# Two-block transformer kernel, one core: the boundaries between stages and the linear attention in another order of work

## The chip, the cores and the metric

The kernel runs on one core of one Trainium2 chip. The metric is device microseconds of one execution. The engines have the profile's names: PE is TensorE (matmuls), ACT is ScalarE, DVE is VectorE, POOL is GpSimd, and SP is SyncE, which here issues most of the transfers from HBM.

## What is computed

Two transformer blocks of width 1024 over 512 tokens, batch 1. The first is FFN, gated linear attention beside forgetting attention, FFN; the second is FFN, sparse attention (NSA) beside retention, FFN, with a last norm. Cut to the parts at issue:

```python
def rmsnorm(x, g):
    y = x * lax.rsqrt(jnp.mean(x * x, axis=-1, keepdims=True) + EPS)
    return y * g
def swiglu(h, w_gu, w_dn):
    g, u = jnp.split(h @ w_gu, 2, axis=-1)      # 1024 -> 2 x 2816 -> 1024
    return (jax.nn.silu(g) * u) @ w_dn
# gla_chunked(q, k, v, log_a), of each head and chunk of 64 tokens
    b = jnp.cumsum(gi, axis=2)
    diff = b[:, :, :, None, :] - b[:, :, None, :, :]
    decay = jnp.exp(jnp.where(causal, diff, -jnp.inf))
    A = jnp.einsum('bhtd,bhsd,bhtsd->bhts', qi, ki, decay)
    o = o_inter + jnp.einsum('bhts,bhse->bhte', A, vi)
# token_mixer
    log_a = jax.nn.log_sigmoid(a_low @ w_a2 + b_a) / GLA_TAU
    o_a = rmsnorm(o_a, g_gla) * jax.nn.silu(r_a)
# second_block
    h = h + 0.5 * gt1 * swiglu_2(modulate(rmsnorm_2(h, norm1_w), sh1, sc1), ...)
```

## The kernel before

**Layout and weights.** x is held transposed, 128 partitions x 8 tiles (KT) x 512 tokens; y and xr share its scratch with h_hi and h_lo. The weights come as 420 slabs of 128 x 8 x 128 fp32 (512 KB). A product is made of three passes of fp32r: h_hi by w_hi, h_lo by w_hi, h_hi by w_lo, so 24 matmuls of 512 columns for a slab and a whole output tile. For each slab SP fetches `raw` (`fetch`), ACT rounds it (`high`, L552, writes w_hi), POOL subtracts (`low`, L510, writes w_lo), and PE waits for `lo_done`. All four engines go through the slabs by number, and each waits by a count, so they must agree on the order. There are four buffers in turn (RING), and two spare ones (SPARE) for slabs head+1 and head+2 of each later stage. `freed_by` says which slab must be used up before a buffer is written again.

**Stages.** STAGES = ffn, mix1, ffn, ffn, mix2, ffn. A stage begins with `head` (two slabs k step by k step, as fast as h_hi and h_lo come, for half the tokens, then two more slabs, then the same for the second half), and ends with `out_tiles`: PLAIN[b] = 7 or 6 whole output tiles, three slabs each in an FFN and one in a mix, then the rest in two halves of 256 tokens.

**Boundaries.** Boundary b stands between stage b-1 and stage b. For b = 1, 2, 3 (TWO) the output is first normed (squares in ssacc and sq, summed over partitions on PE by `sum_out`, ACT's square root `std`, DVE's `recip`, PE's `spread` of the result over partitions), added to x (`post`), and the new x is normed again (squares by ACT in y, added up over the eight tiles by POOL's `sum_squares`, L520, one matmul pair for each half in PE's `sum_new`, L1715). Boundaries 4 to 6 have one norm. Then DVE scales x (L1124), ACT makes h_hi (`split_h`, L582), DVE h_lo (L1133). The factors of the modulation (`pre`, DVE L1102 and L1113) are computed at the boundary.

**mix1.** The first slab holds nar: 16 rows for the decay of all heads and 16 for the forget gates. `decay_logits` makes the four heads' logits, ACT copies them with a bias to `lax` (L720) and takes log sigmoid of all four in one piece (L723 to L728, lt). DVE turns them into cumulative sums per chunk (`decay`, L1268 and L1270). A head of the linear attention takes six slabs (gq, gk, two of vt, two of sr, the gate). The decay within a chunk of 128 is factored over seven block sizes (LEVELS): DVE takes differences for each level (`gla_distances`, L1333, L1334), ACT one Exp over all seven (`gla_exponentials`, L783), DVE multiplies by q and k (L1349, L1350), PE makes the scores of one level after the other (L1895), and DVE picks out of each what belongs to the level (L1367, adiag). PE's slabs of the next head stand between those as filler (`interleaved`). The head's output is normed (osq, osum, L1374; PE L1927; ACT L832; DVE L1376) and gated (oa_hi, ACT L837; oa_lo, DVE L1391).

**Order.** Nothing schedules: every engine's program is written out by hand, waits are on semaphores' counts, and each engine works strictly in order. The SP queue carries the slabs in order; in `mix1` and `mix2` ACT issues the constants' transfers.

## Time and profile before

| | us |
|---|---|
| median of 3 runs | 2761.14 (2757.67 to 2764.49) |
| the profiled run's own time | 2758.52 |
| its span | 2756.7 |
| PE busy | 2636.0 (96%) |
| DVE, POOL, ACT busy | 1170.4, 1045.6, 997.9 |
| mean granted clock of PE | 0.976 of full |

The page of the profile gives busy times and shares of the span. Its share for PE says how little is left; where the idle time stands is read from the list of PE's waits, and what the clock was from the table of stretches. A timeline lists one engine's instructions with start and duration; in brackets stands how long the engine had been idle before and what released it.

### The profile page before, as it was taken

To read this page: it belongs to the slowest core of one execution; us is meant where nothing else is said; L and a number is where in the kernel's file an instruction comes from. 1 tells how busy PE (TensorE), PEld (TensorE's weight loads), DVE (VectorE), ACT (ScalarE), POOL (GpSimd) and SP (SyncE) were. 2 spreads that over 40 slices of the span, in tenths; PEclk is the share of its full clock that TensorE was granted. 3 is DMA by queue.
4 is the path that set the end of the run, shared out by engine and by line. 5 is a ranking of instruction groups with operands and counts; after the bars stand their busy time and mean duration, and the time that the engine had idled before them with its cause. 6 is when DMAs were issued, how large, how long until landed. Compare 5 with 4: busy or idle time off the path is not lost.

```text
span 2756.7 us, 36017 instructions
## 1 busy us (share of the span) xinstructions
PE 2636.0 (96%) x12868; PEld 2135.4 (77%) x12868; DVE 1170.4 (42%) x2091; ACT 997.9 (36%) x1577; POOL 1045.6 (38%) x460
## 2 busy tenths in 40 slices
PE   6999997999999999999998999999999999999998
PEld 4788886777777688888888888888666667888887
DVE  6645225665444225644315553122444456522212
ACT  4222335343454444333324322222454335322221
POOL 0444452233333245444444544452121224344443
PEclk9999997999999899999999999998999999999999
DMA  6655331112222234355532554332111222232332
GB/s 262 213 187 197 126 107 42 54 62 78 84 84 84 79 97 138 115 193 196 175 106 87 191 195 137 100 121 77 44 43 61 83 71 92 77 98 92 99 106 93
DMA packets 78569, 313.31 MB, mean 114 GB/s; under 512 B 9072, under 2 KB 11888, under 8 KB 69008
## 3 DMA queue, kind: packets, MB, share of 16 engines
q1 hardware_dynamic: 64368, 234.91, 25.8%
q10 hardware_dynamic: 14112, 77.17, 7.9%
q8 instruction: 61, 1.00, 0.2%
q14 instruction: 28, 0.23, 0.0%
HBM read 309.91 MB, written 2.13 MB: 113 GB/s over the span
## 4 chain that ended last, share of the span: by engine, by line
PE 79%; DVE 11%; issue 6%; ACT 3%; DMA 1%; POOL 1%; ACTq 0%; DVEq 0%; SPq 0%; POOLq 0%
PE bank L1689 22%; PE bank L1691 22%; PE bank L1690 22%; PE bank L1728 2%; PE bank L1730 1%; PE bank L1729 1%; DVE h_lo L1133 1%; PE pair L1961 1%; PE bank L1971 1%; PE bank L2116 1%; PE bank L1979 1%; DVE adiag L1367 1%; DVE lev L1349 1%; ACT h_hi L582 1%; PE bank L2100 1%
## 5 line engine op out<-in xcount | busy, mean ns | idle before, releaser
L510 POOL TENSOR_TENSOR w_lo<-raw,w_hi 128x1024 fp32r<-128x1024 f32 x414 | 1014.6, 2453 | 1649.6 <-ACT w_hi L552 1589.5
L1689 PE MATMUL bank<-h_hi,w_hi 128*128 128x512 f32 x2064 | 834.9, 405 | 25.1 <-DVE lev L1350 11.5
L552 ACT ACTIVATE w_hi<-raw 128x1024 fp32r<-128x1024 f32 x420 | 444.4, 1059 | 1140.1 <-PE bank L1691 1105.6
L1691 PE MATMUL bank<-h_hi,w_lo 128*128 128x512 f32 x2064 | 807.4, 391 | 0.0
L1690 PE MATMUL bank<-h_lo,w_hi 128*128 128x512 f32 x2064 | 806.3, 391 | 0.0
L1689 PEld LDWEIGHTS bank<-h_hi,w_hi 128*128 128x128 f32 x2064 | 390.3, 189 | 120.0 <-issue 16.5
L1691 PEld LDWEIGHTS bank<-h_hi,w_lo 128*128 128x128 f32 x2064 | 388.9, 188 | 83.1
L1690 PEld LDWEIGHTS bank<-h_lo,w_hi 128*128 128x128 f32 x2064 | 390.0, 189 | 77.6 <-issue 4.1
L1689 PE MATMUL bank<-act_hi,w_hi 128*128 128x512 f32 x616 | 239.6, 389 | 0.0
L1690 PE MATMUL bank<-act_lo,w_hi 128*128 128x512 f32 x616 | 239.6, 389 | 0.0
L1691 PE MATMUL bank<-act_hi,w_lo 128*128 128x512 f32 x616 | 239.6, 389 | 0.0
L1235 DVE TENSOR_TENSOR prod<-bank,rstd 128x512 f32<-128x512 f32 x87 | 60.1, 691 | 412.9 <-PE bank L1691 407.9
L1239 DVE TENSOR_TENSOR act_lo<-prod,act_hi 128x512 f32 (+1 forms) x88 | 178.7, 2031 | 84.8 <-ACT act_hi L677 84.8
L1087 DVE SCALAR_TENSOR_TENSOR adaw<-adaw,silu_c 128x1024 f32<-128x1024 f32 x128 | 178.1, 1426 | 3.9 <-DMA adaw<-ada_dram 3.9
L1182 DVE TENSOR_TENSOR ssacc<-ssacc,sq 128x512 f32<-128x512 f32 x34 | 84.8, 2493 | 206.6 <-ACT sq L599 206.5
L1728 PE MATMUL bank<-h_hi,w_hi 128*128 128x256 f32 (+1 forms) x360 | 116.5, 324 | 28.7 <-DVE h_lo L1645 15.2
L1689 PEld LDWEIGHTS bank<-act_hi,w_hi 128*128 128x128 f32 x616 | 115.6, 188 | 24.2
L1691 PEld LDWEIGHTS bank<-act_hi,w_lo 128*128 128x128 f32 x616 | 115.6, 188 | 24.0
L1690 PEld LDWEIGHTS bank<-act_lo,w_hi 128*128 128x128 f32 x616 | 115.6, 188 | 23.7
L1729 PE MATMUL bank<-h_lo,w_hi 128*128 128x256 f32 (+1 forms) x360 | 111.5, 310 | 0.0
L1730 PE MATMUL bank<-h_hi,w_lo 128*128 128x256 f32 (+1 forms) x360 | 111.2, 309 | 0.0
L1728 PEld LDWEIGHTS bank<-h_hi,w_hi 128*128 128x128 f32 x360 | 73.7, 205 | 41.8 <-DVE h_lo L1133 19.3
(387 smaller groups left out, 3085.7 us busy)
## 6 DMA issues: line engine op xcount, KB each, us to landing
raw<-slabs_dram SPq DMA_DIRECT2D x420, 512.0 KB, 3.5
adaw<-ada_dram ACTq DMA_DIRECT2D x62, 1024.0 KB, 6.9
ada<-ada_dram SPq DMA_DIRECT2D x8, 1024.0 KB, 20.3
x<-xt_dram SPq DMA_DIRECT2D x4, 512.0 KB, 7.8
adaw<-ada_dram SPq DMA_DIRECT2D x2, 1024.0 KB, 24.4
fneg<-fneg_scratch ACTq DMA_DIRECT2D x4, 512.0 KB, 3.5
sq<-fneg_scratch ACTq DMA_DIRECT2D x4, 512.0 KB, 3.4
w<-w_dram ACTq DMA_DIRECT2D x1, 2048.0 KB, 8.6
```

What stands on the lines that cost most here:

```text
L510: nc.gpsimd.tensor_tensor(wl[s][:], raw[s][:], wh[s][:], ALU.subtract).then_inc(lo_done, 1)
L552: nc.scalar.activation(wh[s][:], raw[s][:], ACT.Copy).then_inc(hi_done, 1)
L1087: V.scalar_tensor_tensor(rows, rows, 1.0, silu_c[:, b], ALU.mult, ALU.mult, accum_out=mod[:].rearrange("p b j -> p (b j)")[:, ds(at, 1)])\
L1182: V.tensor_tensor(ssacc[:], ssacc[:], sq[:, t % 2], ALU.add).then_inc(ssadd, 1)
L1235: V.tensor_tensor(prod[:], (acc[(m + 1) % 2] if n else bank(m + 1))[:], sg[:], ALU.mult)\
L1239: V.tensor_tensor(act_l[:, ds(j, 1)].rearrange("p a t -> p (a t)"), prod[:], act_h[:, ds(j, 1)].rearrange("p a t -> p (a t)"), ALU.subtrac ...
L1689: MM(out, wh[s][:, k], a, start=first and j == 0, stop=False)
L1690: MM(out, wh[s][:, k], b, start=False, stop=False)
L1691: ins = MM(out, wl[s][:, k], a, start=False, stop=end and j == len(tiles) - 1)
L1728: MM(out, wh[s][:, k], a, start=start, stop=False)
L1729: MM(out, wh[s][:, k], b, start=False, stop=False)
L1730: return MM(out, wl[s][:, k], a, start=False, stop=stop)
```

## The change

A. `EARLY` and `order()`: slabs head+1 and head+2 of each later stage are fetched, rounded and subtracted before the last six slabs of the stage ahead, where that is an FFN, and before its last two, where it is a mix. Their places in the count move with them.

B. POOL adds the new squares of tiles 0 to 4 (four adds instead of seven, each half), and PE sums the rest: eight matmuls of one column instead of two.

C. At boundaries 1 to 3 PE's sum for the second half of the out norm, and its spread, move from ahead of the head into its k loop. ACT's squares, splits and square roots are put in another order to fit, DVE's `pre` goes to the start of `out_tiles`. At the other boundaries `split_h` goes ahead of the slab rounding and the sums come some groups later.

D. Start of mix1: gq comes right after nar; head 0's log sigmoid is done alone and first, the other three heads' later, its scans between the picks; the constants of both mixes are issued by SP between two slabs.

E. The seven levels have a count each: seven Exps of 512 elements instead of one of 3584, DVE and PE wait for each level. In a head, DVE computes osum before the next head's distances, and ACT the next head's Exps after the square root instead of before it.

F. In mix2 DVE waits for the constants after ks_lo instead of before.

```diff
+EARLY = {c: 2 if kind.startswith("mix") else 6 for (_, c, _, _), (kind, _, _, _) in zip(plan(STAGES)[0][1:], plan(STAGES)[0])}
+def order(c, n=0):
...
+    for head, early in EARLY.items():
+        if head - early <= c <= head:
+            return c + SPARE
+        if head < c <= head + SPARE:
+            return c - 1 - early
+    return c
...
             def sum_squares(b, half):
-                hc, done = halves(half), 14 * (b - 1) + 7 * half
-                for n in range(KT):
+                hc, done = halves(half), 8 * (b - 1) + 4 * half
+                for n in range(KT - 3):
...
                 if TWO[b]:
-                    now = 5 if per > 1 else 4
+                    now = KT if per > 1 else 5
                     new_squares(b, 0, range(now))
-                    out_halves(b, c, m, 1)
...
+                    std(ev + 1, 4)
+                    if per > 1:
+                        out_halves(b, c, m, 1)
+                    split_h(b, 0, range(0, 3))
+                    std(ev + 2, 2)
+                    split_h(b, 0, range(3, 5))
                     high(c + 3)
-                    split_h(b, 0)
+                    split_h(b, 0, range(5, KT))
                     new_squares(b, 1)
...
             def sum_new(b, half):
...
+                for n in src:
+                    pe.wait_ge(sx_done, 8 + 16 * (b - 1) + 8 * half + n + 1)
...
                 if TWO[b]:
-                    sum_out(b, 1)
-                    spread(ev + 1, 2, ST)
                     sum_new(b, 0)
-                    spread(ev + 2, 4, SC1)
+                    spread(ev + 1, 4, SC1)
...
+                        if half == 0 and TWO[p] and k == 1:
+                            sum_out(p, 1)
+                        if half == 0 and TWO[p] and k == 5:
+                            spread(ev + 2, 2, ST)
...
+            def gla_exponentials(i, levels=range(len(LEVELS))):
+                for l in levels:
+                    act.wait_ge(g_lev_diff, len(LEVELS) * i + l + 1)
+                    nc.scalar.activation(lev[:, l], lev[:, l], ACT.Exp).then_inc(g_lev_exp, 1)
...
                 if ahead:
+                    gla_exponentials(i + 1, range(0, 4))
                     gla_key(c + 6, m + 6, i + 1)
+                    gla_exponentials(i + 1, range(4, len(LEVELS)))
...
-                if ahead:
-                    gla_distances(i + 1)
                 dve.wait_ge(g_osq, 2 * i + 2)
                 if i:
                     dve.wait_ge(g_osum, i)
                 V.tensor_tensor(osum[:], osq[:, 0], osq[:, 1], ALU.add).then_inc(g_osum, 1)
+                if ahead:
+                    gla_distances(i + 1)
...
             def mix2(c, m, _):
-                dve.wait_ge(m2_in, 96)
                 dve.wait_ge(n_kh, 1)
                 V.tensor_tensor(ksl[:], bank(m + 2)[:], ksh[:], ALU.subtract).then_inc(acc_free[m % 2], 1)
+                dve.wait_ge(m2_in, 96)
```

How the order moves at three places (numbers behind tile names are buffers). ACT at the boundary from the first FFN to mix1, before: the last output tile's second half (the second L620), the eight squares of the new x (y<-x, L630), the three square roots (L574), and the head's rounding.

```order
L620 ACTIVATE sq<-bank 128x256 [waits half_done,ssadd]
L623 ACTIVATE y<-bank,small 128x256
L574 ACTIVATE small<-bank,small 128x2 [waits s_sum]
L630 ACTIVATE y<-x 128x256 [waits x_done] x5
L620 ACTIVATE sq<-bank 128x256 [waits slab_done]
L623 ACTIVATE y<-bank,small 128x256
L630 ACTIVATE y<-x 128x256 [waits x_done] x2
L574 ACTIVATE small<-bank,small 128x2 [waits s_sum]
L630 ACTIVATE y<-x 128x256 [waits x_done]
L574 ACTIVATE small<-pair,small 128x2 [waits s_sum]
L552 ACTIVATE w_hi_59<-raw_57 128x1024 [waits raw_in1]
```

The same place after:

```order
L661 ACTIVATE y<-x 128x256 [waits x_done] x8
L602 ACTIVATE small<-bank,small 128x2 [waits s_sum]
L651 ACTIVATE sq<-bank 128x256 [waits slab_done]
L654 ACTIVATE y<-bank,small 128x256
L610 ACTIVATE h_hi<-pair,mod 128x256 [waits u_done]
L610 ACTIVATE h_hi<-bank,mod 128x256 [waits u_done]
L610 ACTIVATE h_hi<-pair,mod 128x256 [waits u_done]
L602 ACTIVATE small<-bank,small 128x2 [waits s_sum]
L610 ACTIVATE h_hi<-bank,mod 128x256 [waits u_done]
L610 ACTIVATE h_hi<-pair,mod 128x256 [waits u_done]
L580 ACTIVATE w_hi_59<-raw_57 128x1024 [waits raw_in1]
```

All squares of the new x and their square root now stand ahead of the out tile's second half; that half's square root and the rounding stand within the split. PE at the same boundary, before: the sum of the out norm's second half (L1706), its spread (L1723), the sum of the new squares (L1715), its spread, the head's first matmul.

```order
L1706 MATMUL bank<-ones,ssacc 128x1 [waits sqh_done,ssadd]
L1706 MATMUL bank<-ones,sq 128x1
L1706 MATMUL bank<-ones,ssacc 128x1
L1706 MATMUL bank<-ones,sq 128x1
L1723 MATMUL bank<-ident,small 128x128 [waits rcol_done]
L1723 MATMUL bank<-ident,small 128x128
L1715 MATMUL pair<-ones,y 128x1 [waits sx_added]
L1715 MATMUL pair<-ones,y 128x1
L1723 MATMUL pair<-ident,small 128x128 [waits rcol_done]
L1723 MATMUL pair<-ident,small 128x128
L1728 MATMUL bank<-h_hi,w_hi_56 128x256 [waits lo_done,h_done]
```

After:

```order
L1765 MATMUL bank<-ones,y 128x1 [waits sx_done,sx_added]
L1765 MATMUL bank<-ones,y 128x1
L1765 MATMUL bank<-ones,y 128x1 [waits sx_done]
L1765 MATMUL bank<-ones,y 128x1
L1765 MATMUL bank<-ones,y 128x1 [waits sx_done]
L1765 MATMUL bank<-ones,y 128x1
L1765 MATMUL bank<-ones,y 128x1 [waits sx_done]
L1765 MATMUL bank<-ones,y 128x1
L1773 MATMUL pair<-ident,small 128x128 [waits rcol_done]
L1773 MATMUL pair<-ident,small 128x128
L1778 MATMUL bank<-h_hi,w_hi_56 128x256 [waits lo_done,h_done]
```

Eight one-column matmuls over four tiles of squares stand where two over the added-up tile stood, and the out norm's sum and spread are gone from here; they now follow the second and the sixth k step of the head. ACT at the start of mix1, before: from the logits of all heads to the levels' Exp.

```order
L723 ACTIVATE lt_104<-lax 128x2048 [waits la_x]
L724 ACTIVATE lt_104<-lt_104 128x2048 [waits act_chain]
L725 ACTIVATE nar<-nar 16x512 [waits act_chain]
L726 ACT_TABLE_LOAD
L726 ACTIVATE lt_104<-lt_104 128x512 [waits act_chain]
L727 ACTIVATE lt_104<-lt_104 128x1536
L728 ACTIVATE nar<-nar 16x512
L699 ACTIVATE gq<-bank 128x512 [waits slab_done]
L552 ACTIVATE w_hi_59<-raw_57 128x1024 [waits raw_in1,slab_done]
L699 ACTIVATE vt<-bank 128x512
L783 ACT_TABLE_LOAD
L783 ACTIVATE lev<-lev 128x3584 [waits g_lev_diff]
```

After, two pieces of the same place:

```order
L740 ACTIVATE nar<-bank 48x512 [waits slab_done]
L734 ACTIVATE gq<-bank 128x512 [waits slab_done]
...
L748 ACTIVATE lax<-pair,cols 128x512 [waits la_ready]
L752 ACTIVATE lt_104<-lax 128x512 [waits la_x]
L753 ACTIVATE lt_104<-lt_104 128x512 [waits act_chain]
L754 ACT_TABLE_LOAD
L754 ACTIVATE lt_104<-lt_104 128x512 [waits act_chain]
...
L823 ACTIVATE lev<-lev 128x512 [waits g_lev_diff] x7
L828 ACTIVATE eq<-cs 128x512
L830 ACTIVATE ek<-cs 128x128 x4
L769 ACT_TABLE_LOAD
L769 ACTIVATE lt_104<-lt_104 128x1536
```

gq and head 0's log sigmoid moved to the front, the levels' Exp comes in seven, and the log of the other heads stands behind it, with a table load of its own.

## Rows read from the trace of the kernel before

**Rows 1.** The page: busy time of each engine, and SP's fetches (KB each, us to landing).

```profile
PE 2636.0 (96%) x12868; PEld 2135.4 (77%) x12868; DVE 1170.4 (42%) x2091; ACT 997.9 (36%) x1577; POOL 1045.6 (38%) x460
...
raw<-slabs_dram SPq DMA_DIRECT2D x420, 512.0 KB, 3.5
```

**Rows 2.** PE's waits: what it waited for, us in total, times, longest us.

```profile
PE bank L1689 <- DVE lev L1350: 11.5, 2, 10.3
PE bank L1728 <- DVE h_lo L1133: 11.1, 9, 1.6
...
PE pair L1927 <- DVE osum L1374: 5.3, 4, 1.9
PE bank L1689 <- ACT gq L699: 5.2, 1, 5.2
...
PE bank L1689 <- DVE ks_lo L1441: 2.8, 1, 2.8
```

**Rows 3.** Stretches: us, busy PE, PEld, DVE, ACT, POOL (instructions), clock, DMA share, GB/s.

```profile
402.70:429.30 26.60, 19.49 (x126) 18.35 (x125) 14.11 (x39) 12.21 (x29) 9.66 (x11) 0.81 0.08 28
429.30:497.20 67.90, 52.06 (x265) 43.33 (x266) 37.31 (x74) 34.12 (x43) 13.76 (x6) 0.82 0.16 50
...
2366.80:2389.50 22.70, 18.58 (x132) 18.61 (x133) 10.83 (x22) 6.12 (x14) 4.58 (x2) 0.85 0.16 47
```

**Rows 4.** Timeline of PE at boundary 1: start, us, instruction [idle before <-releaser].

```profile
406.39 0.60 PE L1715 MATMUL pair<-ones,y 128*128 128x1 f32 x4 [0.82 <-POOL y L520]
...
410.17 0.58 PE L1728 MATMUL bank<-h_hi,w_hi 128*128 128x256 f32 x1 [1.61 <-DVE h_lo L1133]
```

**Rows 5.** Timeline of POOL at boundary 1.

```profile
403.88 2.45 POOL L520 TENSOR_TENSOR y<-y 128x256 f32<-128x256 f32 x3 [1.80 <-ACT y L630]
```

**Rows 6.** Timeline of ACT at the start of mix1.

```profile
440.79 1.26 ACT L720 ACTIVATE lax<-pair,cols 128x512 f32<-128x512 f32 x2
...
450.51 1.91 ACT L723 ACTIVATE lt<-lax 128x2048 f32<-128x2048 f32 x1
...
455.05 1.28 ACT L726 ACT_TABLE_LOAD   x1
...
459.02 0.60 ACT L699 ACTIVATE gq<-bank 128x512 f32<-128x512 f32 x1
...
466.53 3.20 ACT L783 ACTIVATE lev<-lev 128x3584 f32<-128x3584 f32 x1 [4.04 <-DVE lev L1334]
```

**Rows 7.** Timeline of DVE at the start of mix1.

```profile
457.81 1.23 DVE L1270 TENSOR_TENSOR_SCAN lac<-segm,lt 128x512 f32<-128x512 f32 x1
...
460.88 2.59 DVE L1333 TENSOR_TENSOR lev<-cs 128x256 f32<-128x256 f32 x1
463.40 0.41 DVE L1334 TENSOR_TENSOR lev<-cs 128x256 f32<-128x256 f32 x1
463.73 0.41 DVE L1333 TENSOR_TENSOR lev<-cs 128x256 f32<-128x256 f32 x1
```

**Rows 8.** Timeline of PE at the start of mix1.

```profile
459.67 0.79 PE L1689 MATMUL bank<-h_hi,w_hi 128*128 128x512 f32 x1 [5.19 <-ACT gq L699]
...
485.00 1.05 PE L1895 MATMUL pair<-lev 128*128 128x128 f32 x8
```

**Rows 9.** Timelines of PE and ACT in head 1's second part (osum, oa_hi).

```profile
563.60 1.13 PE L1927 MATMUL pair<-osum,ones 128*128 128x512 f32 x2 [1.11 <-DVE osum L1374]
...
571.84 1.24 ACT L837 ACTIVATE oa_hi<-og 128x512 fp32r<-128x512 f32 x2 [3.46 <-DVE og L1386]
```

**Rows 10.** Timelines of POOL, DVE and PE at boundary 5.

```profile
2361.51 7.52 POOL L510 TENSOR_TENSOR w_lo<-raw,w_hi 128x1024 fp32r<-128x1024 f32 x3 [3.04 <-ACT w_hi L552]
...
2364.39 2.37 DVE L1102 TENSOR_TENSOR mod<-mod,cols 128x16 f32<-128x16 f32 x1
...
2370.92 0.56 PE L1706 MATMUL bank<-ones,ssacc 128*128 128x1 f32 x2 [4.12 <-ACT sq L620]
```

**Rows 11.** Timeline of ACT at boundary 4.

```profile
1856.60 1.06 ACT L552 ACTIVATE w_hi<-raw 128x1024 fp32r<-128x1024 f32 x1 [5.85 <-DMA raw<-slabs_dram]
```

200 lines of the change are left out of this document (112 added, 88 removed).

## The prediction

> **What bounds the kernel now.** I read first the page's line of busy times [rows 1]: PE (TensorE) is busy 2636.0 of 2756.7 us, 96%. So a change can win at most the 121 us in which PE stands still, plus what PE loses where the granted clock is below full. The second view is PE's waits [rows 2]: they are small and stand where a stage begins. Two belong to the start of the linear attention (11.5 for the levels, 5.2 for the query), one to the boundaries between stages (h_lo, 11.1), one to the linear attention's heads (osum, 5.3), one to the start of mix2 (2.8). The third view is the busy time by stretches [rows 3]: the first boundary and the start of mix1 run at a granted clock of 0.81 and 0.82, the boundary before the last FFN at 0.85, so behind an idle PE come matmuls at the lower of its two levels, 1.2 GHz instead of 2.4. A stall there costs its own length and some more. Everything the diff edits lies in such places; elsewhere PE is fed and stays fed.
>
> **Boundaries 1 to 3 (two norms; parts B and C of the change).** Before, PE's last output tile is followed by seven POOL adds for the new squares; the last three take 2.45 us [rows 5], PE waits 0.82 for them before its sum at 406.39, then comes the spread, and the head's first matmul starts at 410.17 after 1.61 more of waiting on h_lo [rows 4]. After, the first half's squares are complete before the last output tile ends: POOL adds four and not seven, and PE goes straight to its sum. The POOL adds (2.45), the sum of the out norm and the second spread leave that path: 2.4 to 3.2 us. What comes in their place: PE's sum is 8 matmuls where there were 2 (the four records of the row at 406.39 took 0.60, so 16 records about 1.9: +1.3); the spread of the out norm now sits in the head's k loop, and ACT's square root for it stands ahead of split tile 3, so ACT waits until PE has done the first two k steps (six matmuls of 256 columns each; +1.6 at full clock, +3.6 at the lower); a reciprocal (+0.15), and the slab rounding of 1.06 [rows 11], now in the middle of the split (tiles 3 and 4 ahead of it). Second half: three POOL adds less (2.6 by the same row), 1.3 of matmuls more. A boundary gives between -1.0 and +1.3. The clock, low there before, decides which. I take 0 for the three together, with -4 to +4 as the bounds.
>
> **Early slabs (part A).** The roundings of slabs head+1 and head+2 (1.06 on ACT [rows 11], 7.52 for three or 2.5 on POOL [rows 10]) move from the end of the out tiles to before the last six slabs (FFN) or two (mix). They lie there beside PE-bound slabs: ACT is busy 36%, POOL 38% [rows 1]. The cost is zero as long as SP's two fetches have landed, for ACT works in order and its next rounding queues behind. If that cover is gone it costs what the transfer is late. SP's queue: the two spare fetches wait for nothing now, and go ahead of the last ones. Gain: boundary 5, below; at boundary 4 ACT waited 5.85 for a raw slab and the split stood behind it [rows 11]. Split now goes first, and of that about 1.6 us was on PE's path: **-1.6**. (End of the kernel: the same freed order, -0.5, bounds -1 and 0.)
>
> **Start of mix1 (parts D and E), the largest term.** ACT before: the squashing of all four heads' gate logits in one piece of 2048 elements, 1.91 for Abs and as much for Exp, then a table load of 1.28, and only then the log of head 0, gq at 459.02, while PE waits 5.19 for gq [rows 6, 8]. DVE's scan of head 0 starts at 457.81 [rows 7]; its 14 level differences follow at 0.34 us a piece (463.40 to 463.73), one of them held to 2.59; ACT's one Exp over seven levels starts at 466.53 and takes 3.20 [rows 6]. DVE meanwhile does the other heads' logs and scans, then the 14 products, and PE gets the levels after 10.3 of waiting, the longest of that group [rows 2]; its third score (the row of eight records) is at 485.00 [rows 8].
> After, step by step from the same durations, a piece of 512 elements on ACT being 0.6 as gq's was [rows 6]: gq directly after nar, so PE doesn't wait for it (5.19 gone). The first logits stand at 440.79 [rows 6]; logit, Abs, Exp, load and Ln of head 0 alone are 0.6 x 4 + 1.28, with gq ahead done at 444.8. DVE: log 0.7, scan 1.23, a copy, so the first pair of differences at 447.9 and, 14 by 0.34, the last at 452. ACT: three more logits, then the first value tile when PE has it, about 450.7 (it stood just ahead of the row at 450.51). Abs and Exp of the other three heads by three quarters of 1.91 each, a load, three pieces for the forget gate: 457.1. Rounding and second value tile: 458.7. Seven Exps of 512 elements, 0.57 each (3.20 in one before, +0.8), until 462.7, each released to DVE as it is done; eq and the four pieces of ek until 464.5; DVE's work from there to the first pick (qp, kp, the chunk tiles, two vtok copies, a pick) about 4.5. The third score comes at about 469.1 and not 485.0: -15.9. Against this: the other heads' logs and scans (three scans of 1.23 and a log of 1536 elements, some 5.4 of DVE) are now between the picks, of which about 1 stays on the path, and one POOL roundings' collision with DVE more, +1. Sum **-14**, with -11 and -18 as ends. From the other side: the two stalls are 15.5, some 3 us of lower clock go with them, and I expect PE to stand about 4 at the first pick.
> The table loads are where a page speaks against this change. Here a load took 1.28 us [rows 6], and the new order makes one more of them (Ln, Exp, Ln); the first is hidden, by the sum above, since PE's slabs bound ACT until 450.7. The Trainium skill, page "ScalarE: Activation LUTs", section "Table sets: the hidden batching unit", puts a switch at about 2.7 us and wants work batched by set; by that figure two loads ahead of the levels would lose up to 2.8 more and the term be -11, an estimate from the page. The trace's 1.28 disagrees, and the measurement decides.
>
> **Heads 1 to 3 (part E).** osum goes ahead of the next head's distances on DVE: PE waited for it four times, 5.3 us in all [rows 2], 1.11 in the second head [rows 9]; three of these go, -3.3. Head 1 gets its scan earlier, -2.0. Against it: the next head's Exps now stand between the square root and oa_hi on ACT, in which ACT before only waited 3.46 for og [rows 9]; DVE's lo part waits on oa_hi, and its products wait for nothing that it doesn't do itself. Levels 0 to 3, gk, 4 to 6, eq, ek are about 6.7 us in a gap of 3.5 plus 2: the first pick comes about 1.0 later in each of heads 2 and 3, and 1.0 in the last: +3. PE then waits about 3 us at a pick; if its clock falls behind that, 2 to 3 us more in each head, which I put at +4 in all. Sum **+2**, ends -2 and +9.
>
> **Start of mix2 (parts D and F).** DVE waited for the constants' transfer before ks_lo, and PE 2.8 for that [rows 2]. Now the wait stands behind ks_lo, and the transfers are issued by SP between its fetches of slabs first+5 and first+6. In SP's queue they stand behind a fetch whose buffer is free once the last out tile is done, long before ks_lo, and the two fetches behind them come six small issues later, with five slabs of PE's time still ahead of them: **-2.8**, ends -2.8 and 0. The same holds for mix1's two (lmask, segm), which ACT issued before. What is queued behind the moved wait is the compression's cab, needed much later.
>
> **Boundary 5.** DVE's small adds of the modulation, one of 16 columns for 2.37 us [rows 10] and one of 8 behind it, ran beside three roundings of POOL back to back (7.52 [rows 10]); they held back the new x, its squares, and PE's sum, for which PE waited 4.12 [rows 10]. Now pre() stands at the start of the out tiles and the spare roundings are done early. PE's sum moves from its second to its sixth group and no longer waits: -4.1, and of the lower clock in this stretch (22.7 us at 0.85 [rows 3]) about 2.1: **-6.2**, ends -4 and -7.
>
> **Sum.** 0 - 1.6 - 0.5 - 14 + 2 - 2.8 - 6.2 = -23.1. The profiled run took 2758.52 (span 2756.7), so 2735.4 by its own measure; the three runs' median is 2761.14, 2.6 above it, which gives **2738**.
>
> **Rivals.**
> A, more than forecast: the boundaries' -1.0 each holds, the lower clock there goes too (a stretch of 26.6 us at 0.81 at boundary 1 [rows 3]; 1 us each of it), and mix1 gives -18: boundaries three times -2, so -6; mix1 -4; heads at -2 instead of +2, -4; 14 less, 2724, and with the kernel's end at -1, 2723. For it: a stall that goes takes low clock with it. Against: the new sums keep a gap of some 4 us at each boundary.
> B, the heads take it back: pick chain +1 to +2 a head and three low-clock stretches (+9), mix1 only -11: 10 more than forecast, 2748. For it: ACT's added 6.7 us stand on the way to oa_hi, and PE's waits there were short before.
> C, slower: DVE and POOL exclude each other. A difference of 256 columns took 2.59 where its neighbours take 0.34 [rows 7], an add of 16 columns 2.37 [rows 10]: each time a rounding ran on POOL. In the new order DVE has its level work strewn through the whole head, six roundings fall into a head, and each could land on the path: four more collisions in each of 4 heads at 2.3 are +36.8, so 2738 + 36.8 = 2775. It decides from 14 collisions more than now (2761 + 8.3 - 2738 = 31 us, over 2.3). Against: DVE's work is the same number of instructions, and only those ahead of a pick count; before, about two of six collide.
> The Trainium skill, page "SBUF — State Buffer", section "Who interferes with whom", says that VectorE and GpSimd share a port pair as an exclusive lock, held for the whole instruction by whoever began. The trace's 2.59 agrees.
> D, the early roundings starve a mix tail: ACT would wait in order for spare slabs; a fetch takes 3.5 us in the median (the row of raw), and PE 2636.0/420 = 6.3 us a slab [rows 1], so three in a row could be late; 5 us at each of the five boundaries would give 2763, no change. Against: six slabs of lead in the FFN tails; only the two mix tails are tight.
>
> **How the numbers follow.** Forecast 0.57, A 0.17, B 0.18, C 0.03, D 0.05. The range takes A and B in: 2723 to 2753 (B with boundaries at +4), and leaves out about 0.2. About 0.3%, 8.3 us, is what a measurement can tell from no change; the forecast, A and B (2748 is -0.5%) are all faster, less a tail of B: faster 0.91, within it 0.06 (D and that tail), slower 0.03 (C).
>
> **What would show it.** In the profile after: PE's wait on gq gone, and that on the levels 4 us or less instead of 11.5; the third score some 14 us earlier against the stage's start than now; ks_lo's wait gone; no wait on the squares at boundary 5 and its granted clock near 1; at boundaries 1 to 3 the stretch from that sum to the head's first matmul much as before (3.8), no wait for POOL ahead of it, but a wait for h_lo at the third or fourth tile; in heads 1 to 3 no wait on osum, one on adiag of about 3 us instead. It is wrong if DVE has many more level instructions of over 2 us than now (C), or ACT idles on raw slabs in a mix tail (D).

## The result, and the profile after

| | before | changed |
|---|---|---|
| median, us | 2764.49 (5 runs, 2757.67 to 2769.85) | 2737.11 (5 runs, 2734.56 to 2739.73) |
| ratio | | 0.991 (0.9893 to 0.9927) |
| the profiled run's own time | 2758.52 | 2737.11 |
| span | 2756.7 | 2735.3 |
| PE busy | 2636.0 (96%) | 2642.1 (97%) |

Forecast were 2738 and a gain of 23.1 us in the profiled run; it was 21.4. The page of the changed kernel, its line of busy times (before: [rows 1]):

```profile
PE 2642.1 (97%) x12940; PEld 2145.9 (78%) x12940; DVE 1156.3 (42%) x2091; ACT 1001.9 (37%) x1604; POOL 1037.2 (38%) x442
```

PE's waits in the changed kernel (waited for: us in total, times, longest; before: [rows 2]):

```profile
PE pair L1948 <- DVE adiag L1413: 15.9, 4, 5.8
PE bank L1778 <- DVE h_lo L1693: 14.0, 7, 7.3
PE bank L1778 <- DVE h_lo L1172: 12.0, 11, 1.6
...
PE pair L1980 <- DVE osum L1420: 1.9, 1, 1.9
```

The waits on the levels (11.5), on gq (5.2) and on ks_lo (2.8) are gone, that on osum fell from four times to one. A new one heads the list: 15.9 us for DVE's picks; before, the picks made PE wait three times for some 4 us in all.

Where the time went can be read more sharply than from the medians. Both kernels run the same 10728 slab matmuls in the same order, so a stretch can be cut from the start of one matmul to the start of another, the same two in both traces. The stretches of the kernel before (window: us, busy PE, PEld, DVE, ACT, POOL with instructions, granted clock, DMA share, GB/s): boundary 1 from the last out tile's second half to the matmul behind the decay logits; from there to the slab matmul behind head 0's cross terms, with four groups of scores still to come; the rest of head 0 and heads 1 to 3; the FFN behind boundary 2 with boundary 3; the start of mix2; the end of mix2 with boundary 5.

```profile
395.65:443.65 48.00, 40.51 (x264) 35.48 (x262) 24.77 (x67) 23.00 (x49) 18.95 (x18) 0.88 0.19 61
443.65:488.60 44.95, 29.50 (x134) 25.39 (x133) 27.98 (x52) 21.68 (x24) 7.42 (x3) 0.75 0.11 35
488.60:643.12 154.52, 144.55 (x765) 120.54 (x763) 108.79 (x190) 64.96 (x85) 51.78 (x18) 1.00 0.19 62
1125.65:1500.66 375.01, 368.81 (x1774) 311.50 (x1774) 158.69 (x206) 118.76 (x165) 177.53 (x82) 0.99 0.46 157
1862.23:1890.89 28.66, 24.86 (x189) 22.27 (x189) 10.05 (x25) 11.50 (x21) 5.42 (x3) 1.00 0.36 126
2042.76:2383.74 340.98, 326.78 (x1576) 239.12 (x1575) 172.48 (x329) 141.41 (x247) 107.54 (x44) 0.97 0.24 78
```

The same six in the changed kernel:

```profile
398.75:444.19 45.44, 41.31 (x286) 37.39 (x284) 24.85 (x67) 22.19 (x49) 12.91 (x11) 0.92 0.19 64
444.19:474.08 29.89, 25.52 (x133) 22.42 (x133) 24.75 (x48) 24.64 (x34) 7.47 (x4) 0.89 0.16 53
474.08:633.05 158.97, 147.39 (x765) 124.74 (x763) 111.24 (x195) 66.44 (x103) 54.46 (x18) 0.97 0.18 60
1115.30:1489.84 374.54, 370.75 (x1797) 313.33 (x1798) 158.54 (x206) 118.64 (x165) 172.56 (x76) 1.00 0.45 157
1849.34:1874.69 25.35, 24.46 (x190) 22.13 (x188) 8.65 (x21) 11.19 (x20) 7.82 (x4) 1.00 0.35 128
2028.22:2362.14 333.92, 323.86 (x1576) 236.29 (x1575) 166.00 (x325) 139.72 (x244) 105.74 (x43) 0.98 0.24 79
```

| place | forecast, us | measured, us |
|---|---|---|
| boundaries 1, 2, 3 | 0 (-4 to +4) | -2.6, +0.3, -0.5 (the last with the FFN ahead of it): -2.8 |
| start of mix1, to the slab matmul behind head 0's cross terms | -14 (-18 to -11) | -15.1 |
| rest of head 0, heads 1 to 3 | +2 (-2 to +9) | +4.4 |
| boundary 4 | -1.6 | -2.1 |
| start of mix2 | -2.8 | -3.3 |
| boundary 5 | -6.2 (-7 to -4) | -7.1 |
| end | -0.5 | -0.3 |
| where nothing was moved | 0 | +3.1 ahead of boundary 1, -0.6 in mix1's second part, +1.7 in mix2's middle, +0.5 behind the last slab |

The cut between boundary 4 and mix2 lies inside the head: 0.5 of the 3.3 us is still boundary 4's, and 2.8 is the wait for ks_lo.

The last row is what one execution differs from another by: a lower clock that came at a place or didn't. The stretch ahead of boundary 1 took 369.6 to 372.4 us in the profiles of the kernel before and two kernels near it, and 370.1 to 373.7 in those of the changed kernel and ten near it. Without this row the edits gave -26.3, against -23.1 forecast and -27.4 between the medians. What the boundaries' row owes to the same spread is told in the part on why the prediction was right.

### The profile page after: what moved, and what is told of

Read it like the earlier page. It is cut to its first block, busy times and chain, and to the rows that moved or that the text cites. A ratio compares the mean times of both kernels' runs of the same rounds, so it can differ in the third digit from the quotient of the medians.

```text
span 2735.3 us, 36041 instructions
## 1 busy us (share of the span) xinstructions
PE 2642.1 (97%) x12940; PEld 2145.9 (78%) x12940; DVE 1156.3 (42%) x2091; ACT 1001.9 (37%) x1604; POOL 1037.2 (38%) x442
## 4 chain that ended last, share of the span: by engine, by line
PE 85%; DVE 7%; issue 5%; ACT 3%; POOL 0%; DMA 0%; DVEq 0%; ACTq 0%; POOLq 0%
PE bank L1737 23%; PE bank L1739 23%; PE bank L1738 22%; PE bank L1778 2%; PE bank L1779 2%; PE bank L1780 2%; PE pair L1948 1%; PE pair L2014 1%; PE bank L2024 1%; PE bank L2032 1%; PE bank L2169 1%; DVE h_lo L1172 1%; DVE lev L1397 1%; DVE lev L1396 1%; PE bank L2153 1%
## 5 line engine op out<-in xcount | busy, mean ns | idle before, releaser
L1275 DVE TENSOR_TENSOR prod<-bank,rstd 128x512 f32<-128x512 f32 x87 | 60.1, 691 | 417.4 <-PE bank L1739 411.7
```

The lines of the kernel that those rows point to most:

```text
L1275: V.tensor_tensor(prod[:], (acc[(m + 1) % 2] if n else bank(m + 1))[:], sg[:], ALU.mult)\
```

## The experiments

Twelve kernels, on the same measure: by place, against the kernel before or the changed one. For the start of mix1 I read the distance from the first decay logit to the last score of head 0 (the matmul of gq and gk): 439.20 to 494.25 in the kernel before, so 55.0, and in the changed kernel 39.2 by these rows of PE's timeline:

```profile
440.56 1.98 PE L1886 MATMUL pair<-nar,wa 16*128 16x512 f32 x4
...
461.12 1.07 PE L1948 MATMUL pair<-lev 128*128 128x128 f32 x8
462.73 1.06 PE L1948 MATMUL pair<-lev 128*128 128x128 f32 x8
468.85 2.04 PE L1948 MATMUL pair<-lev 128*128 128x128 f32 x8 [4.37 <-DVE adiag L1413]
...
479.73 1.05 PE L1948 MATMUL pair<-gq,gk 128*128 128x128 f32 x8
```

**One Exp for seven levels.** Rival theories: the levels in turn carry the gain, or the early start of head 0's chain does.

```diff
                 for l in levels:
-                    act.wait_ge(g_lev_diff, len(LEVELS) * i + l + 1)
-                    nc.scalar.activation(lev[:, l], lev[:, l], ACT.Exp).then_inc(g_lev_exp, 1)
+                    if l == 0:
+                        act.wait_ge(g_lev_diff, len(LEVELS) * (i + 1))
+                        nc.scalar.activation(lev[:], lev[:], ACT.Exp).then_inc(g_lev_exp, len(LEVELS))
```

> The changed kernel with one edit undone: ACT takes the seven levels in one Exp of 3584 elements again, after all differences, in every head. I read the stretch from the decay logits' first matmul to the last score of head 0 (the one of gq and gk): 55.0 us in the kernel before, 39.2 in the changed one. Theory (the time of mix1's start came from starting head 0's chain earlier, and the levels in turn are worth little, because DVE's differences are done at 455.6 and ACT is free for the Exps only at 458.3, so all a single Exp loses is the overlap of DVE's products with it): the products begin about 2.5 us later, the last score 1 to 2 us later, 40 to 41. Rival (the levels in turn are what carries the gain): 45 or more. In heads 1 to 3 both expect little, up to 1 us a head, for the levels' Exps there are hidden beside the normalisation. Whole run +1 to +3 us by the theory, +8 or more by the rival.

Measured: 440.86 to 484.69, 43.8 us, so 4.7 more, between what the two said; 2739.9 us in one run. The Exp starts at 458.58 and takes 3.19, as I had it; the third score is only 3.5 later against the logits (31.8 instead of 28.3). The remaining 1.2 lie behind a wait of 6.51 us: two groups of scores at the lower clock (2.05 and 1.91 us, where 1.05 is the normal; in the changed kernel, behind 4.37 us, it is 2.04 and 1.15):

```profile
472.66 2.05 PE L1949 MATMUL pair<-lev 128*128 128x128 f32 x8 [6.51 <-DVE adiag L1414]
475.79 1.91 PE L1949 MATMUL pair<-lev 128*128 128x128 f32 x8
479.93 1.05 PE L1949 MATMUL pair<-lev 128*128 128x128 f32 x8
```

**The four heads' log sigmoids together.**

```diff
-                logits(0)
-                act.wait_ge(la_x, 1)
...
-                for h in range(1, HG):
+                for h in range(HG):
                     logits(h)
...
-                chain.link(nc.scalar.activation(lt4[:, 1:HG], lax[:, 1:HG], ACT.Abs))
-                chain.link(nc.scalar.activation(lt4[:, 1:HG], lt4[:, 1:HG], ACT.Exp, scale=-1.0))
+                chain.link(nc.scalar.activation(lt4[:], lax[:], ACT.Abs))
+                chain.link(nc.scalar.activation(lt4[:], lt4[:], ACT.Exp, scale=-1.0))
...
+                nc.scalar.activation(lt4[:, 0], lt4[:, 0], ACT.Ln, bias=1.0).then_inc(la_l, 1)
```

> The changed kernel with one edit undone: the log sigmoids of the four heads are taken together again, after the first value tile; gq stays early and the levels stay in turn. Theory (head 0's log alone is the largest piece): its log is ready at about 457 instead of 446, the first difference at 459.5, and from there the pipelined levels need some 13 us to the first pick, so the last score of head 0 comes 4 to 6 us later: 43 to 45 us from the logits instead of 39.2. Rival (the gain is all in not waiting for gq): within 1 us of 39.2. Rival with the levels in turn as the carrier: also within 2 us.

Measured: 438.98 to 489.68, 50.7 us: 11.5 more, twice what I expected; 2745.42 us. Against the logits DVE's first log is 12.3 us later (17.9 instead of 5.6 behind them). In the changed kernel DVE waits 2.8 us for the first Exp, and that is all the slack there is: 9.5 come through, and the lower clock behind PE's waits (7.79 for the levels, 3.74 at the third score) goes with the rest. I had assumed 5 to 7 us of slack.

**gq late.**

```diff
-                gla_query(c + 1, m + 1, 0, ahead=False)
...
                 c, m = c + 1, m + 1
+                gla_query(c, m, 0, ahead=False)
                 gla_value(c, m, 0, 1)
```

> The changed kernel with one edit undone: ACT takes gq out of its bank only after the first value tile and the other heads' Exp, as before, so PE cannot begin the second value slab until then. Theory: PE waits 3 to 5 us for the bank at the second value slab, whose tile then comes as much later; ACT's level Exps stand behind that tile, so the whole chain moves by it: last score 42 to 44 us from the logits instead of 39.2. Rival (that wait was in the shadow of the levels' chain and giving it up costs nothing, since PE waits for the first pick anyway): 39 to 40.

Measured: 442.35 to 482.79, 40.4 us: 1.3 more; 2740.8 us, with 1.8 of the difference standing already ahead of the logits, most of it in boundary 1's head at a clock of 0.76. PE waits 3.19 for the bank, just as expected, and then doesn't wait at the first pick at all (4.37 in the changed kernel). That is close to the rival's 39 to 40 and not the theory's 42 to 44: with the other edits in place that wait stood in the shadow of DVE's chain. In the prediction I had credited it with 5.2 us in my check of the sum.

**The other heads' scans ahead of head 0's products.**

```diff
+                nc.scalar.activation(lt4[:, 1:HG], lt4[:, 1:HG], ACT.Ln, bias=1.0).then_inc(la_l, 1)
+                nc.scalar.activation(nar[32:48, :], nar[32:48, :], ACT.Ln, bias=1.0).then_inc(la_l, 1)
                 c, m = c + 1, m + 1
                 gla_value(c, m, 0, 1)
                 gla_exponentials(0)
...
-                gla_head(c, m, 0, True, others())
+                for _ in others():
+                    pass
+                gla_head(c, m, 0, True)
```

> The changed kernel with one edit undone: the other heads' logs are taken on ACT ahead of the second value tile, and DVE makes their logs and scans ahead of head 0's products, as before, instead of between the picks. Theory (5.4 us of DVE and some 4.5 of ACT with a table load go back onto the chain; part of it runs side by side): last score 45 to 46 us from the logits instead of 39.2. Rival (it was hidden where it stood): within 1.5 us of 39.2. If the four undone edits together give back clearly more than 15.9 us, they overlap and no single one can be credited with the gain.

Measured: 439.73 to 488.83, 49.1 us: 9.9 more; 2750.14 us. More than expected again, and again with waits of 5.68 and 3.68 and the lower clock behind them. Taken singly the four edits give back 4.7 + 11.5 + 1.3 + 9.9 = 27.4 us where all together won 15.9. So none of them owns the gain: they shorten one chain (logits, log, scan, differences, Exp, products, cross terms, first pick), and each of them missing puts back what it saves of that chain, less the slack in it. Where PE's wait grows, matmuls at the lower clock follow (1.2 us with one Exp, some 2 with the logs together). No run has any of the four alone in the kernel before.

**Boundary 5, DVE's additions alone**, in the kernel before:

```diff
             def out_tiles(b, c, m, per, pieces=()):
+                if b < LAST:
+                    pre(b)
...
             def boundary(b, c, m, per):
                 ev = EVENTS[b]
-                if b < LAST:
-                    pre(b)
```

> The kernel before with one part of the change alone: DVE's additions for the modulation move from the boundary to the start of the out tiles; nothing else. Theory (at the boundary before the last FFN these two small additions, 2.4 and 2.3 us beside POOL's roundings, held back the new x and with it PE's sum): PE's wait of 4.1 us there shrinks to at most 1.5, and the same matmuls behind it come 3 to 6 us earlier against the kernel before, with the lower clock in that stretch gone. Rival (POOL's three roundings in a row, which stay where they are in this kernel, hold back DVE's next additions instead): 0 to 2 us, PE still waits 2.5 or more. Elsewhere no change.

Measured: PE's wait there went from 4.12 to 1.16, and the matmuls behind it came 4.4 us earlier (2.9 late ahead of it, 1.5 early once the half is done, by the same matmuls in both traces). Elsewhere differences came and went with the clock, the largest 3.2 us in the middle of mix2 (0.90 against 0.92). One run gave 2758.17, beside 2759.14. The new x starts at once after PE has ended its half, though POOL's three roundings stand there as before:

```profile
2364.40 7.52 POOL L510 TENSOR_TENSOR w_lo<-raw,w_hi 128x1024 fp32r<-128x1024 f32 x3 [3.04 <-ACT w_hi L552]
...
2369.02 0.88 DVE L1195 SCALAR_TENSOR_TENSOR x<-bank,small,x 128x256 f32<-128x256 f32 x2 [1.66 <-PE bank L1730]
...
2370.85 0.35 PE L1706 MATMUL bank<-ones,ssacc 128*128 128x1 f32 x2 [1.16 <-ACT sq L620]
```

**Boundary 5, the sum's place alone**, in the kernel before:

```diff
-                                if half and done == 2:
+                                if half and done == (2 if TWO[b] else 6):
                                     sum_out(b, 0)
-                                if half and done == 5:
+                                if half and done == (5 if TWO[b] else 9):
                                     spread(ev, 0, SC1)
```

> The kernel before with another part alone: at the boundaries with one norm PE's sum of the first half's squares stands behind its sixth group of matmuls instead of its second, the spread behind the ninth instead of the fifth. Theory: four groups of three matmuls of 256 columns are 1.4 us of work that PE does instead of waiting, so its wait at the boundary before the last FFN goes from 4.1 to 2.5 to 3, and 1.5 to 2.5 us are won there. Rival (the place of the sum is what mattered there, and the clock stays up once the wait is short): 4 us or more. At the boundary before mix2 and at the end at most 0.5 each.

Measured: the wait is 2.71, and 1.4 us are won there by the same matmuls, just the work that PE now does ahead of the sum and a little under the expected; another 0.7 at the end of the kernel (2756.64 beside 2759.14). The two alone make 5.8, the changed kernel had 7.1. The prediction's two causes hold. The last 1.3 come only with both together or with the early roundings: the clock at this place was 0.85 in the kernel before, 0.84 here, 0.93 with the additions moved, and 1.00 in the changed kernel. No run has both edits without the early roundings.

**POOL adds seven again**, in the changed kernel:

```diff
-                for n in range(KT - 3):
+                for n in range(KT):
...
-                t0, src = HALF * half, range(KT - 4, KT)
+                t0, src = HALF * half, range(KT - 1, KT)
```

> The changed kernel with one part undone: POOL adds up all eight tiles of new squares again and PE sums one tile with two matmuls, for both halves of the three boundaries with two norms. Theory (it traded about as much as it took): PE waits some 1.2 us for POOL ahead of its sum at each, but the sum takes 0.6 instead of 1.8 us, so the head's first matmul comes within 0.7 us of the changed kernel's at each of the three, and the second half's too; whole run within 2.5 us. Rival (taking POOL off the path is what brought the head forward by 3 us): the head's first matmul comes 1.5 to 3 us later at each.

Measured: 2745.4 us, 8.3 slower. The head's first matmul comes 1.1, 2.0 and 0.6 later at the three boundaries, counted from the out tiles ahead, and the head's first half, which holds the second sum, is 1.3, 0.8 and 1.7 longer: the theory was wrong and the rival nearer. PE now waits six times for POOL, 14.1 us, where the changed kernel waits 1.2 and the kernel before 7.8:

```profile
PE bank L1765 <- POOL y L546: 7.7, 3, 4.3
...
PE pair L1765 <- POOL y L546: 6.4, 3, 2.2
```

An explanation that no run tests by itself: in the kernel before, part of POOL's adding ran while PE did the out norm's sum and spread; with these moved into the head, PE has nothing to do meanwhile.

**The boundaries in the old order**, PE's part of the sum of squares kept:

```diff
                 if TWO[b]:
+                    sum_out(b, 1)
+                    spread(ev + 1, 2, ST)
                     sum_new(b, 0)
-                    spread(ev + 1, 4, SC1)
+                    spread(ev + 2, 4, SC1)
...
-                        if half == 0 and TWO[p] and k == 1:
-                            sum_out(p, 1)
-                        if half == 0 and TWO[p] and k == 5:
-                            spread(ev + 2, 2, ST)
```

(and ACT's and DVE's order as in the kernel before)

> The changed kernel with one part undone: at the three boundaries with two norms the order of ACT, DVE and PE is the old one again (the out norm's sum for the second half and its spread ahead of the new squares' sum and ahead of the head, one rounding ahead of the split), while POOL still adds only five tiles and PE sums the rest. From the last matmul of the out tiles to the head's first it was 7.7 us in the kernel before and 4.7 in the changed one at the first boundary. Theory: that distance becomes 7.5 to 8.5, but the head, which PE's own matmuls bound at the lower clock, loses the 2.3 us of sum and spread that had moved into it, so each boundary costs 0 to 1.5 us more than in the changed kernel, the run 1 to 5 us more. Rival (the new order was no gain at all, PE work that moves into a PE-bound head is paid there in full and the lower clock with it): the run is as fast as the changed kernel or up to 3 us faster.

Measured: 2735.88 us in one run, and 1.2 us earlier than the changed kernel at the last matmul. The head's first matmul comes 3.3, 3.7 and 3.2 us later at the three boundaries, and all of it is back before the head's first half is done. Head's first matmul to the second half's first at boundaries 1 and 2 in this kernel (clock 0.90 and 0.91; 14.3 us at 0.85 at the third):

```profile
412.54:429.66 17.12, 15.53 (x116) 15.34 (x116) 12.28 (x34) 8.21 (x19) 3.24 (x5) 0.90 0.00 1
1095.67:1112.70 17.03, 15.44 (x116) 15.21 (x116) 12.28 (x34) 8.21 (x19) 3.25 (x5) 0.91 0.00 1
```

and the same two in the changed kernel (0.83 and 0.76; 17.2 us at 0.91 at the third):

```profile
410.01:430.61 20.60, 18.99 (x128) 18.31 (x128) 12.55 (x35) 9.36 (x21) 5.36 (x5) 0.83 0.02 5
1092.94:1115.30 22.36, 20.75 (x133) 20.39 (x133) 12.54 (x35) 9.36 (x21) 5.34 (x5) 0.76 0.00 1
```

The head in the new order is longer by more than the 2.2 us of sum and spread that moved into it (1.56 at 412.18 and 0.6 at 418.72), and the clock isn't the reason: seven profiles of kernels with the new order and four adds took 20.6 to 21.8 us for it at boundary 1, at a granted clock of 0.76 to 0.92, and the one at 0.92, the kernel with one Exp, took 20.66 against the changed kernel's 20.60 at 0.83. What fills the time at the higher clock stands in the part on why the prediction was right. So the new order of the boundaries won nothing, and rather lost. Cut from the last 54 matmuls of the out tiles to the head's second half, the three boundaries together took 101.7 to 103.4 us in the profiles of the kernel before and its two single edits, 100.6 (the changed kernel) to 102.5 in those seven, and 99.1 and 98.9 in the two kernels with the old order and four adds. What won something there is among what this kernel keeps, POOL's fewer adds, the early `pre` and the early slabs, which I didn't separate further. For POOL's adds alone the run before this one is evidence only together with the new order.

**The first picks ahead of the cross terms**, in the changed kernel, since the picks are what PE now waits for. `cross` is the work on qp, kp, k0 and qc and `tokens` a vtok copy, both ahead of pick 0 until here:

```diff
                 for l in range(len(LEVELS) + 1):
...
+                    if l == 1:
+                        cross()
+                    if l in (2, 3):
+                        tokens(l - 2)
-                    if then and l:
+                    if then and l >= 3:
                         next(then, None)
```

> The changed kernel with one addition: in each head of the linear attention DVE takes the first two picks right behind the levels' products, and does the work for the cross terms (qp, kp, k0, qc) after the second pick and the two vtok copies after the third and fourth, instead of all of it ahead of the first pick. Theory (PE's four waits for the first pick, 15.9 us in all, are this DVE work and its collisions with POOL's roundings standing ahead of the pick, while PE needs it only at its fourth score): the four waits fall to 5 us or less in sum, PE waits up to 1.5 us a head for the cross terms, and the run gets 6 to 12 us faster than the changed kernel. Rival (the chain only shifts: the same DVE work then stands ahead of the third pick and PE waits for it there): 0 to 3 us.

Measured: 2724.37 us, 12.7 less than the changed kernel; the waits for picks are two, 4.0 us. A new one of 2.52 stands ahead of head 0's output, where the scans now crowd the last picks.

**DVE's other work into its idle places.**

```diff
-                gla_head(c, m, 0, True, others())
-                dve.wait_ge(la_l, 3)
...
+                gla_head(c, m, 0, True, others)
+                for i in range(1, HG):
+                    gla_head(c + 6 * i, m + 6 * i, i, i < HG - 1, forget if i == 1 else None)
...
             def gla_head(c, m, i, ahead, then=None):
...
+                if then:
+                    then()
                 dve.wait_ge(g_osq, 2 * i + 2)
```

> The version with the first picks ahead of the cross terms (12.7 us faster than the changed kernel in one look), and DVE's other work moved out of the chain: the other heads' logs and scans behind head 0's last pick, and the forget gate's scan behind head 1's last pick, where DVE stood idle for 6.8 us each time, waiting for the squares of the head's output. Theory (what PE still waits for in these two heads is that work, 2.5 us ahead of head 0's output and 2.7 at head 1's third score, with some lower clock behind each): both waits under 1 us and 4 to 7 us less than with the picks alone, so some 17 to 20 us below the changed kernel. Rival (the next head's distances then start later by what is left over of the 5.4 us, and POOL's roundings collide with the scans there): 0 to 2 us less than with the picks alone.

Measured: 2718.97 us (2716.09 to 2721.94, 4 runs), ratio to the kernel before 0.984 (0.9824 to 0.9857). Against the version with the picks alone, heads 0 and 1 gained 4.5 and 3.0 us by the same matmuls, and both waits are gone. The times are 5.4 apart, though the profiled execution itself lost 5.5 of the 7.4 again behind the heads, most of it in mix2, where the two kernels are equal.

**Five adds, six matmuls**, on top of it:

```diff
-                for n in range(KT - 3):
+                for n in range(KT - 2):
...
-                t0, src = HALF * half, range(KT - 4, KT)
+                t0, src = HALF * half, range(KT - 3, KT)
```

> The version just named, with POOL adding up six tiles of new squares (five adds) and PE summing two of the rest and that sum with six matmuls instead of eight, at the three boundaries with two norms. Theory: at the first boundary POOL's fifth add ends at the time at which PE's out tile ends, so PE waits for nothing and the sum is 0.46 us shorter, twice at each of three boundaries: 1 to 3 us less than without it. Rival (the fifth add is late wherever a collision with DVE falls, as the seven adds cost 8 us in the run that undid this part): 1 to 4 us more.

Measured: 2720.58 us (2717.7 to 2723.32), ratio 0.9846 (0.983 to 0.9863): no gain that can be told. By the same matmuls it was 0.7 late at the end, having been 1.0 early ahead of boundary 1, with one wait of 2.6 us for POOL and three of 0.5: the shorter sum was eaten where an add came late.

**The old order of the boundaries with it all**, four adds again:

```diff
                 if TWO[b]:
+                    sum_out(b, 1)
+                    spread(ev + 1, 2, ST)
                     sum_new(b, 0)
...
                 for l in range(len(LEVELS) + 1):
...
+                    if l == 1:
+                        cross()
...
+                if then:
+                    then()
                 dve.wait_ge(g_osq, 2 * i + 2)
```

> The fastest version so far (picks first, the scans in DVE's idle places; 2718.97 us) with the old order of the three boundaries with two norms, POOL still adding only five tiles. Undoing that order in the changed kernel brought the head's first matmul 3.2 to 3.7 us later at each boundary, and yet it ended 1.2 us earlier. Theory (deferring the out norm's sum into the head is worth nothing, since the head is bound by PE's own matmuls and pays for what moves into it): 2714 to 2719, equal or up to 4 us faster. Rival (the single look was luck of the clock's lower level in those heads, and the deferral is worth its 3 us at full clock): 2722 to 2728.

Measured: 2716.57 us (2714.21 to 2718.6, 5 runs), ratio 0.9833 (0.982 to 0.9847), the fastest of all: 20.5 below the changed kernel and 2.4 below the version with the new order, whose runs overlap with its own (2714.21 to 2718.6 and 2716.09 to 2721.94). What was expected of deferring the sum holds: equal or a little faster without it, and the rival's 2722 to 2728 is excluded.

## Why the prediction was right

**Total.** 2738 against 2737.11, in the range. The nearness is partly luck: the terms of the table are off by up to 2.8, mostly toward more gain, while the 4.7 us of the last row went the other way, and the median of before moved from 2761.14 to 2764.49 with more runs.

**Start of mix1.** The term (-14, measured -15.1) and its steps held: the third score was to come at 469.1 and came at 468.85; the levels' Exps at 458.7, came at 458.27; PE's wait at the first pick about 4, was 4.37. The clock times flatter it a little, for the changed kernel's logits began 1.4 us later (440.56 and 439.20). Counted from the logits, the third score was forecast at 29.9 and came at 28.3, the Exps at 19.5 and at 17.7, and head 0's log at 5.6 and at 5.5. One size on the way was wrong and cost nothing, because ACT and not DVE was late: the last difference came at 15.0 and not 12.8, one of them held for 2.62 while POOL rounded. The extra table load took 1.28 like the others (rows of ACT's timeline of the changed kernel):

```profile
444.13 1.28 ACT L754 ACT_TABLE_LOAD   x1
...
453.35 1.28 ACT L764 ACT_TABLE_LOAD   x1
454.64 1.49 ACT L764 ACTIVATE lt<-lt 128x1536 f32<-128x1536 f32 x1
...
458.27 3.74 ACT L823 ACTIVATE lev<-lev 128x512 f32<-128x512 f32 x7
```

The Trainium skill's 2.7 us for a switch ("ScalarE: Activation LUTs", "Table sets: the hidden batching unit") is not what these traces show: every load in them is 1.28, the activation behind the one at 453.35 starts 1.29 after it, and the term of -11 that this figure would have given is the one further from the measured -15.1.

**Boundaries 1 to 3.** The sum of 0 was near the measured -2.8 and within its bounds, and the two steps in it held. "The POOL adds ... leave that path: 2.4 to 3.2 us": the head starts 3.3, 2.9 and 3.1 us sooner behind the out tiles. Against it stood in the head a wait of ACT for its square root, +1.6 us at full clock and +3.6 at the lower. ACT does wait there, and the head's first half is 1.5, 3.3 and 2.7 us longer than in the kernel before. At the first boundary of the changed kernel PE shows no wait from it, since its matmuls run at the lower clock and h_lo comes just in time. At the third the clock is up sooner, and PE waits for h_lo three times (ACT at the first boundary, PE at the third):

```profile
413.91 0.26 ACT L602 ACTIVATE small<-bank,small 128x2 f32<-128x2 f32 x1 [2.66 <-PE bank L1754]
...
1477.71 0.39 PE L1778 MATMUL bank<-h_hi,w_hi 128*128 128x256 f32 x1 [0.42 <-DVE h_lo L1172]
...
1479.19 0.39 PE L1778 MATMUL bank<-h_hi,w_hi 128*128 128x256 f32 x1 [0.50 <-DVE h_lo L1172]
...
1480.50 0.38 PE L1778 MATMUL bank<-h_hi,w_hi 128*128 128x256 f32 x1 [0.33 <-DVE h_lo L1172]
```

The kernel with one Exp has the same three waits at boundary 1 (0.42, 0.51 and 0.34), with the clock at 0.92. So two chains of nearly the same length run through the k loop, PE's matmuls at the lower clock and h_lo behind ACT's square root, and a higher clock shortens the head by little (22.4 us at 0.76 and 21.1 at 0.92 at the second boundary, the latter in the kernel with the logs together). What the prediction left out is that the out norm's sum (1.7 us at 412.18) and its spread (0.6) are PE's own work: I had taken them off the path ahead of the head and counted only ACT's wait in it. How the 3.1 to 5.3 us between the two orders of the head divide between that work and ACT's wait no run shows. The two edits that I summed are also not independent, as the run with seven adds shows (+8.3). And -2.8 is one pair of profiles. The same three stretches together took 462.4 us in the kernel before, 460.8 and 464.9 in its two single edits, 459.7 in the changed kernel and 460.7 to 462.5 in six others with its order and four adds: the changed kernel's is the lowest of these, so a part of the 2.8 is luck.

**Early slabs, boundary 4, end, mix2.** -2.1, -0.3 and -3.3 against -1.6, -0.5 and -2.8, where 0.5 of the last belongs to boundary 4. PE waited for w_lo only in the first FFN (2.9) and behind boundary 3 (0.7, as before), so rival D didn't occur.

**Boundary 5.** -7.1 against -6.2, a little past the end of -7. Both named causes were shown singly (4.4 and 1.4). That the early roundings have a part in it, which the prediction said beside them, is not shown: with DVE's additions out of the way, the three roundings in a row held up nothing that a wait shows, but 1.3 us are left over that only the changed kernel has.

**Heads 1 to 3.** +4.4 against +2, inside the ends. The signs were right (no wait on osum but in the last head, a wait for the pick instead, lower clock), the size of the pick's wait too small for head 1 (5.76 instead of about 3). A collision that I hadn't placed there came on top: DVE's two products og<-og,sr took 3.24 where it had taken 1.29, while POOL rounded.

```profile
500.48 3.24 DVE L1434 TENSOR_TENSOR og<-og,sr 128x512 f32<-128x512 f32 x2
504.44 1.29 DVE L1439 TENSOR_TENSOR oa_lo<-og,oa_hi 128x512 fp32r<-128x512 f32 x2 [0.71 <-ACT oa_hi L879]
...
507.12 2.66 DVE L1330 TENSOR_TENSOR_SCAN nar<-fneg,nar 16x512 f32<-16x512 f32 x1
509.82 2.43 DVE L1331 COPY fneg<-nar 16x512 f32<-16x512 f32 x1
```

That ACT's Exps delay oa_hi was right, and 1.0 a little too much here. The first oa_hi needs only the first og, which was done at 503.12, and it starts at 503.72, when ACT's ek is done; 0.6 in each of the three heads that have a next one. In the kernel with one Exp og isn't held, and there the delay is plain, 2.0 us behind the first og's end at 506.20 (rows of DVE's and ACT's timelines):

```profile
505.50 1.29 DVE L1435 TENSOR_TENSOR og<-og,sr 128x512 f32<-128x512 f32 x2
...
507.00 1.26 ACT L831 ACTIVATE ek<-cs 128x128 f32<-128x128 f32 x4
508.18 1.14 ACT L880 ACTIVATE oa_hi<-og 128x512 fp32r<-128x512 f32 x2
...
508.90 1.31 DVE L1440 TENSOR_TENSOR oa_lo<-og,oa_hi 128x512 fp32r<-128x512 f32 x2 [2.10 <-ACT oa_hi L880]
```

In head 1 the forget gate's scan and copy are held too. What PE waits for is DVE's whole chain up to the first pick; moving its cross terms and scans out of that chain took 18 us off the run, which shows it.

**Rival C**, the lock between DVE and POOL, is real as a price (the rows above) but not as a number: of 112 level instructions 6 took over 2 us before, and 6 after. Their times added up say the same, 58.9 us before and 60.1 after. Rival A's low clock stayed: 0.83, 0.76 and 0.91 in the heads.

## What to carry to other kernels

Where one chain across several engines bounds a stage, cost the chain and not the waits: the wait for gq was 5.2 us long and, beside the other edits, worth 1.3, and four edits that gave back 27 us singly had won 16 together. Work that is moved out of a gap into the next stretch is not hidden by that; ask of each moved instruction whether its new place has idle time on its own engine, and which engine will stand waiting for its result there, as ACT did for the moved sum. After such a change read the list of waits again: the new first line named DVE's picks, and taking the work that isn't needed yet from in front of them won 18 us more.

## What the runs showed of the hardware that was not expected

A wait of PE has an after-effect: in the kernel with one Exp a wait of 6.51 us was followed by two groups of eight scores of 2.05 and 1.91 us instead of 1.05, 1.9 us beyond the wait itself in the scores alone. How much of the lower clock follows an idle place is not settled by the order of the work. The head at boundary 1 had a granted clock of 0.90 in the old order with four adds and 0.83 in the changed kernel, the second 0.91 and 0.76, but the third 0.85 and 0.91, and among the seven profiles with the new order and four adds the first head had anything from 0.76 to 0.92. The same happens in mix2 between executions of equal code: the stretch from 1874.69 to 2028.22 of the changed kernel, 153.5 us at 0.91, took 151.9 us at 0.92 in the kernel with one Exp and 158.2 us at 0.88 in the one with the idle places filled. Which level such a stretch gets is open, and one pair of profiles doesn't tell an edit's effect from it there.
